# Sparse layer: query products between index products, the mask in the first head's sum, one engine for all copies of transposed maps

## The reference

```python
q = (cq @ w_uq).reshape(Bn, S, C_HEADS, C_NOPE + C_ROPE)          # 16 heads of 96
qi = partial_rope((cq @ w_qi).reshape(Bn, S, IDX_HEADS, IDX_DIM), pos)
# for each block of 128 queries:
dots = jnp.einsum('bqhd,bsd->bqhs', qib, ki)                       # 8 index heads
score = jnp.einsum('bqh,bqhs->bqs', wib, jax.nn.relu(dots)) * IDX_DIM ** -0.5
score = jnp.where(causal, score, -jnp.inf)
_, idx = lax.top_k(score, k_sel)                                   # 128 keys for each query
# softmax attention of the 16 heads over the chosen keys alone
```

## Time and profile before

| what | value |
|---|---|
| median of 3 runs | 2972.53 us (2969.16 to 2978.28) |
| the profiled execution's own time | 2973.47 us |
| its span, first to last instruction | 2971.7 us |
| busy share PE, PEld, DVE, ACT | 93%, 78%, 54%, 39% |
| mean granted TensorE clock | 0.97 |
| DMA queue q1 | 198.60 MB, 21.6% of 16 engines' span |

### The profile page before, as it was taken

One profiled execution on the slowest core, in us unless ns is written; L12 is line 12 of the kernel. 1 busy time (PEld: TensorE's weight loads), 2 busy tenths in 40 slices (PEclk: granted clock), 3 DMA queues, 4 the chain that ended last, 5 costly groups with the idle time before them and its releaser, 6 DMA issues.

```text
span 2971.7 us, 39600 instructions
## 1 busy us (share of the span) xinstructions
PE 2760.0 (93%) x15280; PEld 2328.7 (78%) x15280; DVE 1596.2 (54%) x3415; ACT 1155.1 (39%) x2524; POOL 32.0 (1%) x32
## 2 busy tenths in 40 slices
PE   7998999999999899999998989999997689899998
PEld 7888889899888787878776767888775467688886
DVE  5354656555535555555578454444566845534445
ACT  3334332433333532343334543333346354432333
POOL 1000000000000000000000000000000000000000
PEclk9998999999999999999999999999998799999999
DMA  3201212122220111212221122332221011233322
GB/s 126 77 26 41 65 37 79 54 68 87 79 75 26 59 54 48 81 57 94 89 79 47 40 68 87 97 99 93 85 71 38 20 33 43 67 100 98 100 90 89
DMA packets 115260, 205.32 MB, mean 69 GB/s; under 512 B 13824, under 2 KB 23680, under 8 KB 114944
## 3 DMA queue, kind: packets, MB, share of 16 engines
q1 hardware_dynamic: 113920, 198.60, 21.6%
q10 hardware_dynamic: 1152, 4.20, 0.4%
HBM read 200.58 MB, written 2.10 MB: 68 GB/s over the span
## 4 chain that ended last, share of the span: by engine, by line
PE 74%; DVE 15%; ACT 8%; issue 2%; DMA 0%; SPq 0%; DVEq 0%; ACTq 0%
PE pp L1985 19%; PE pp L1987 18%; PE pp L1986 18%; PE pp L2059 5%; PE pp L2035 4%; DVE wl L1552 3%; PE pp L2047 2%; ACT wh L1371 2%; PE pp L1981 1%; PE pp L1982 1%; PE pp L1983 1%; ACT P L1481 1%; DVE P L1775 1%; DVE Z L1912 1%; DVE st L1910 1%
## 5 line engine op out<-in xcount | busy, mean ns | idle before, releaser
L1985 PE MATMUL pp<-Hh,wh 128*128 128x512 f32 (+1 forms) x2304 | 866.4, 376 | 75.0 <-DVE Hl L1574 29.4
L1986 PE MATMUL pp<-Hl,wh 128*128 128x512 f32 (+1 forms) x2304 | 802.2, 348 | 0.0
L1987 PE MATMUL pp<-Hh,wl 128*128 128x512 f32 (+1 forms) x2304 | 801.2, 348 | 0.0
L1552 DVE TENSOR_TENSOR wl<-raw,wh 128x512 fp32r<-128x512 f32 (+2 forms) x774 | 499.7, 669 | 419.5 <-ACT wh L1371 405.9
L1371 ACT ACTIVATE wh<-raw 128x512 fp32r<-128x512 f32 (+2 forms) x774 | 450.7, 604 | 328.8 <-PE pp L1987 274.9
L1985 PEld LDWEIGHTS pp<-Hh,wh 128*128 128x128 f32 x2304 | 448.1, 194 | 164.1 <-DVE wl L1552 36.2
L1986 PEld LDWEIGHTS pp<-Hl,wh 128*128 128x128 f32 x2304 | 448.4, 195 | 53.8 <-issue 6.5
L1987 PEld LDWEIGHTS pp<-Hh,wl 128*128 128x128 f32 x2304 | 446.8, 194 | 52.7
L1985 PE MATMUL pp<-Yh,wh 128*128 128x512 f32 (+1 forms) x1254 | 471.8, 376 | 10.9 <-DVE Yl L1572 5.7
L1987 PE MATMUL pp<-Yh,wl 128*128 128x512 f32 (+1 forms) x1254 | 449.4, 358 | 0.0
L1986 PE MATMUL pp<-Yl,wh 128*128 128x512 f32 (+1 forms) x1254 | 449.3, 358 | 0.0
(11 more groups left out here) (242 smaller groups left out, 2632.2 us busy)
## 6 DMA issues: line engine op xcount, KB each, us to landing
raw<-in_w SPq DMA_DIRECT2D x698, 256.0 KB, 2.6
raw<-in_w SPq DMA_DIRECT2D x36, 192.0 KB, 2.3
raw<-in_w SPq DMA_DIRECT2D x40, 128.0 KB, 2.0
out<-X SPq DMA_DIRECT2D x8, 256.0 KB, 2.0
con<-in_con ACTq DMA_DIRECT2D x1, 1576.0 KB, 11.5
X<-in_x SPq DMA_DIRECT2D x2, 528.0 KB, 5.8
X<-in_x ACTq DMA_DIRECT2D x2, 528.0 KB, 6.9
Z<-in_p ACTq DMA_DIRECT2D x2, 512.0 KB, 3.3
```

Source lines behind the costliest of these rows:

```text
L1552: e.tensor_tensor(part("wl", j), landing(j), part("wh", j).bitcast(F), ALU.subtract).then_inc(*dve.up("split", j))
L1985: e.matmul(it.ps, wh, xh, start=it.first, stop=False)
L1986: e.matmul(it.ps, wh, xl, start=False, stop=False)
L1987: e.matmul(it.ps, wl, xh, start=False, stop=it.end).then_inc(*pe.up())
```

## The change

Three things change. The 18 steps of the first queries are made into a generator ahead of the index stage, and one of them is taken after each index product of blocks 2 and 3 (16 of the 18). Head 0 adds the mask in its own operation, and the separate addition is gone. In the first attention group, ACT copies the transposed maps of even and odd units; all other attention groups keep DVE for even and ACT for odd.

```diff
-    def attend(heads, finish, steps, total, banks=2, slots=None, tail=None):
+    def attend(heads, finish, steps, total, banks=2, slots=None, tail=None, turned_by=("dve", "act")):
...
             do("turn", u=n, qr=qr, p=p, exp=u["exp"], small=small[0][0] if small else None, whole=[c[0] for c in whole], free5=free[5], free4=free[4],
-               pt_free=ptfree[slot], ident=ident, b4=bank(4), b5=bank(5), pt=pt)
+               pt_free=ptfree[slot], ident=ident, b4=bank(4), b5=bank(5), pt=pt, by=turned_by[n % 2])
...
             if whole:
-                free[4] = ("act" if n % 2 else "dve", "turned", n)
+                free[4] = (turned_by[n % 2], "turned", n)
...
+        queries = latent(0, Q, before0)
         rl = [rsS] + [m["P"][:, T * x:T * x + S] for x in (1, 2)]
...
                 do("index", i=i, h=h, ps=bank(bk)[:, 0:ext], q=M[64 * (h % 2):64 * (h % 2) + 64, h, 128 * i:ext], k=(twin if h % 2 else ki)[:, 0:ext], rl=rl[n % 3][:, 0:ext], free=free[bk],
-                   indexed=indexed, taken=relus[n - 3] if n > 2 else None, scale=k2[:, i, h:h + 1], score=sel[:, i, 0:ext])
+                   indexed=indexed, taken=relus[n - 3] if n > 2 else None, scale=k2[:, i, h:h + 1], score=sel[:, i, 0:ext],
+                   mask=causal(ext))
                 relus.append((i, h))
                 free[bk] = ("act", "index", i, h)
-            do("index_mask", score=sel[:, i, 0:ext], mask=causal(ext))
+                if i > 1:
+                    next(queries)
...
-        for steps in (latent(0, Q, before0), values(0, before0)):
+        for steps in (queries, values(0, before0)):
...
             attend(us, finish2(4 * g), beside() if g == 0 else first_half("w_out_c_2", 0, Q, mark(), ("dve", "mark", mark())),
-                   92 if g == 0 else 32, 3)
+                   92 if g == 0 else 32, 3, turned_by=("act", "act") if g == 0 else ("dve", "act"))
...
-            e.tensor_scalar(it.score, it.rl, it.scale, 0.0, ALU.mult, ALU.add).then_inc(*dve.up("index", it.i, it.h))
+            e.scalar_tensor_tensor(out=it.score, in0=it.rl, scalar=it.scale, in1=it.mask, op0=ALU.mult, op1=ALU.add).then_inc(*dve.up("index", it.i, it.h))
...
-    def index_mask(it):
-        dve.wait_ge("dve")
-        e.tensor_tensor(it.score, it.score, it.mask, ALU.add).then_inc(*dve.up())
```

More of the change, by code:

```diff
@@ L389, in product @@
             n = u["n"]
-            do("product", u=n, o=bank(6)[0:u["qr"], u["o"]:u["o"] + u["dv"]], pt=u["pt"], vready=u["vready"], free=free[6] if u["o"] == 0 else None,
+            do("product", u=n, by=turned_by[n % 2], o=bank(6)[0:u["qr"], u["o"]:u["o"] + u["dv"]], pt=u["pt"], vready=u["vready"], free=free[6] if u["o"] == 0 else None,
                small=any(c[1] != 128 for c in u["chunks"]), whole=any(c[1] == 128 for c in u["chunks"]))
@@ L1486, in turn @@
     def turn(it):
-        if it.whole and it.u % 2:
+        if it.whole and it.by == "act":
             act.wait_ge("pe", "turn", it.u)
@@ L1783, in turn @@
             e.tensor_copy(it.pt[:, 512:640], it.b5[:, 0:128]).then_inc(*dve.up("turned small", it.u))
-        if it.whole and it.u % 2 == 0:
+        if it.whole and it.by == "dve":
             dve.wait_ge("pe", "turn", it.u)
@@ L1928, in vector_program @@
             "turn": turn, "divide": divide, "times_z": times_z, "negs": negs, "lambda": lam, "mix": mix, "diff out": diff_out,
-            "diff norm": diff_norm, "diff scale": diff_scale, "index_key": index_key, "index_w": index_w, "query squares": query_squares, "query factors": query_factors, "query scales": query_scales, "index": index, "index_mask": index_mask,
+            "diff norm": diff_norm, "diff scale": diff_scale, "index_key": index_key, "index_w": index_w, "query squares": query_squares, "query factors": query_factors, "query scales": query_scales, "index": index,
             "best8": best8, "choose": choose, "mask there": mask_there}
@@ L2050, in product @@
         if it.whole:
-            pe.wait_ge("act" if it.u % 2 else "dve", "turned", it.u)
+            pe.wait_ge(it.by, "turned", it.u)
         if it.small:
```

## The result

The changed kernel has a median of 2983.56 us over 20 runs (2975.73 to 3001.89), the kernel before, run beside it, 2975.35 (2969.16 to 2995.85). The ratio is 1.0033, with a 95% interval of 1.0016 to 1.0049: slower by 0.33%, or 9.8 us (4.8 to 14.6); the medians themselves are 8.2 us apart.

The account below looks back on a forecast made before the run. DVE was taken to set the time from the index stage to about 2385 us, PE after it. Index stage with mask +4.1, copies -3.7, late copies +0.4 gave +0.8 us: 2973.3 from 2972.53, range 2965.0 to 2980.0.

Parts of the forecast that it names:

- PE's pace in blocks 2 and 3: Index stage: a score product and a step take 1.40 us on 384 keys, 1.62 on 512; part of the +4.1 us.
- a pace 20% slower: Upper end for the index stage: PE's sixteen products and steps take a fifth longer, making +4.1 into +7.5 us.
- the walk: Block 3 followed head by head through PE, ACT and DVE: first round at 2287.5 us, 9.3 later than before.
- the slower one, PE and ACT sharing the pace: Rival, blocks 2 and 3: PE's steps, ACT's heads out and DVE's rotation in a row; 2976.6 to 2981 us, chance 0.09.
- The mask: On DVE's path in the index stage: three additions go, head 0's operation gets longer; -1.0 us, ends -1.4 and -0.8.
- The time given back by the moved steps: After the index stage: one rotation (2.7 us) and five splits (2.5) leave DVE's later work, 5.2 us.
- DVE's wait before head 5: Block 3: DVE waits 2.5 us while ACT makes a pair of copies, a split, heads out and head 5.
- The 3.19 us behind the second rotation: DVE's wait after the second rotation, behind heads out on ACT, was to stay as before, about 3.2 us.
- PE's idle time before the first scores: Sign to check: PE idles some 19 us before the first scores, its `values` steps ending about 2291.5.
- The copies: First attention group up to 2385 us: moving DVE's copies to ACT saves 3.7 us, ends -6.8 and -1.5.
- After the last choice: From 2385 us, with PE the bound: ACT's later copies for units 22 to 30 cost +0.4 us, ends 0 and +3.3.
- the third rival's chain of waits for ACT's copies: First attention group: PE waits for ACT's copy in even units, so copies gain nothing; +7.4 us, 2979.9, chance 0.08.

Follow-up runs that it names:

- `e7_afterpool`: The changed kernel with the latent queries' heads out made by POOL instead of ACT; first index operation to first MAX8 31.93 us against 32.06, one execution.
- `e2_mask`: The kernel before with only the mask added in head 0's operation; ratio 0.9986 (0.9968 to 1.0003) against the kernel before, median 2972.70 us.
- `e4_maskcopies`: The changed kernel without the interleaved query steps, so mask and copies alone; ratio 1.0001 (0.9985 to 1.0017) against the kernel before, median 2976.35 us.

## Why the prediction was wrong

**The step that failed is PE's pace in blocks 2 and 3,** priced at 1.40 us for "a score product of 384 keys and a step", and at 1.62 with 512 keys. That price was read from a product of 96 rows, a neighbour with a step behind it. It was the wrong neighbour: after 96 rows the step's weights load beside the running product, and the step starts 0.41 us after it. After 64 rows they don't, and it starts 0.84 us after. Measured are 1.73 and 1.95 us, 16 x 0.33 = 5.3 us more in all. The bound that I gave, a pace 20% slower, was 1.68 and 1.94, nearly what came, and with it the index part was +7.5; measured are +7.6. The term's bound was right, the value in it was not. (By its own rows the second price is 0.95 + 0.69 = 1.64, not 1.62; the 0.2 us that this makes decided nothing.)

**The end of the walk.** The first MAX8 was to come 28.2 us after the first index operation and came after 32.06. The walk took DVE and ACT as partners of PE; in fact PE alone was the path up to its sixteenth step, and a DVE wait of 2.54 us that the walk charged in full cost nothing (`e7_afterpool`: 31.93). With PE's true price this shows at once: 8 x 1.73 + 8 x 1.95 = 29.4 us, and from 2258.3, where block 2 starts, to 2287.7, where the last product and step end. What was left, 2.4 us, was the last pair of copies and split on ACT and the split on DVE.

**The rival that came nearest** is the slower one, PE and ACT sharing the pace: it said 2290.8 for the first round, 31.5 us after the first index operation of the kernel before, and 32.06 was measured. Its mechanism, ACT's block and the rotation added to PE's time, fell: PE's rows show no standstill in blocks 2 and 3, and without ACT's block the stretch stays (`e7_afterpool`). It was right by its figure and wrong by its reason.

**What was right.** The mask: -1.18 by itself, for -1.0. The time given back by the moved steps: 5.5, for 5.2. DVE's wait before head 5: 2.54, for 2.5. The 3.19 us behind the second rotation. PE's idle time before the first scores: 18.73, for 19.

**The copies** gave -2.3 us in the changed kernel, for -3.7, and -2.1 to -3.0 against the kernel before in the others without POOL and interleaving. Removed were 4.8 us of copies and the waits of 1.96 (before the copy at 2370) and 0.41 (before the scores at 2330.08), 7.2 in all. In their place DVE waits for others at points where it had been late itself: 0.99 and 0.66 us before the low part of the output (0.39 and none before), 0.82 before a split (0.2 before), 1.20 before the reciprocal at 2375.69 and 0.39 before the scores after it. These new waits are 3.5 us; the 1.4 us that are then still missing lie in gaps too short to name. I had the first of them at 0.3, and it is 0.6. The one before the reciprocal is the wait for the product of unit 15, for which I had taken off 2.3 of the 3.7 us. The split and the second low part I had not seen.

**After the last choice** -0.06, for +0.4: PE did have scores in hand, and the third rival's chain of waits for ACT's copies did not come. The +1.40 us in the last stretch, which were not in my sum, are the lower clock, 0.89 against 1.00. PE in order of time after:

```profile
2415.56 0.63 PE L1985 MATMUL pp<-Hl,wh 128*128 128x512 f32 x1
2415.98 0.63 PE L1986 MATMUL pp<-Hh,wl 128*128 128x512 f32 x1
```

and at the same place before:

```profile
2411.53 0.40 PE L1986 MATMUL pp<-Hl,wh 128*128 128x512 f32 x1
2411.76 0.39 PE L1987 MATMUL pp<-Hh,wl 128*128 128x512 f32 x1
```

They follow each other after 0.42 us instead of 0.23, seven times over.

**The sum.** +7.6 - 2.3 - 0.1 + 1.4 = +6.7 us in the profiled pair, for +0.8. Put on the 2975.35 of the runs beside it, this is 2982.0; the median is 2983.56. What is left, 1.5 us, is less than the scatter of the parts outside the stretch, and I can't split it further. Of the 10.3 us between forecast and median 2.8 are thus the base, which stood at 2972.53 over three runs and at 2975.35 over twenty, and 5.9 the forecast itself. On the old base the +6.7 us give 2979.2, just inside the range: that the median falls outside it takes both, and the mechanism was wrong either way.

## What to carry to other kernels

Where a price is taken from the nearest row, ask if that row has the same shape in the array: a step between 64-row products costs 0.38 us more than its own time, and also ends the running of two products side by side, so alternate in pairs or not at all. Work that already lies beside another engine's bound gains nothing by being moved, and it can only turn the engine that carries it into the bound where it lands: compare that engine's idle time there (3.7 us) with what is brought (16 steps of three products, 0.23 us each) first. A copy that blocks a queue can go to an engine that has nothing behind it, even a slower one, if no operation that it slows runs beside it.

## What the runs showed of the hardware

- Changing between 64-row and 128-row products costs PE 0.38 us for both ways, and twice the rows without the change are faster (1.35 against 1.73 us a head and step).
- Four POOL copies of 32x512 float32 within SBUF take 2.60 to 3.93 us (ACT: 2.58). DVE's MAX8 beside them keeps its 0.43 us, but its `scalar_tensor_tensor` on 512 columns takes 0.91 us instead of 0.75, and POOL's single copies beside it 0.96 instead of 0.61 (`e7_afterpool`).
- The time from the second group's first scores to the end, the same instructions in all kernels, is 545.0 to 545.2 us in six profiles, 548.3 in two, and 550.6 to 552.2 in the others. The mean granted clock of that stretch is 0.99 in `e2_mask`, at 545.1, and 0.97 in `e4_maskcopies`, at 552.1. A gain of 3 us in one stage is thus less than what that stretch differs by between two executions.
